# A nine-stage transformer program on one core: retention heads moved into the gate slots, and the first weights and x taken in quarters

## The chip, the core and the metric

The program runs on one core of one Trainium2 chip. The time is the device time of one execution in microseconds (us). The kernel before takes 1748.47 us, the median of three runs (1748.13 to 1749.23). The engines are named as the profile names them: PE is TensorE, DVE is VectorE, ACT is ScalarE, POOL is GpSimd, SP is SyncE, which only starts transfers here.

## The reference

Two models run one after the other on 256 tokens of 1024 features, in float32: two layers (stages F0, A, F1 and F2, B, F3), a final norm (N), and then one layer of a second model with 16 extra tokens in front (R and F4). The stage that changes is the mixer R of the second model:

```python
def _mixer(u, w_in, decay_f, decay_b, gn_w, w_ret_out, q_norm_w, w_uq, kv_norm_w, w_uk, w_uv, w_mla_out, w_o, ...):
    proj = u @ w_in
    rq, rk, rv, rg, a_cq, a_ckv, a_kr, a_gret, a_gmla = jnp.split(proj, SPLIT_IDX, axis=-1)
    rq = _apply_rope(rq...); rk = _apply_rope(rk...) * (RET_DK ** -0.5)
    y_ret = _head_group_norm(_bidir_retention(rq, rk, rv, decay_f, decay_b), gn_w)   # 8 heads of 128 values
    y_ret = (jax.nn.silu(rg) * y_ret) @ w_ret_out
    c_q = _rmsnorm(a_cq, q_norm_w);   q = c_q @ w_uq         # 8 heads: 64 plain and 32 turned features
    c_kv = _rmsnorm(a_ckv, kv_norm_w); k_nope = c_kv @ w_uk; v = c_kv @ w_uv
    y_mla = _mla_attention(q_nope, q_rope, k_nope, k_rope, v) @ w_mla_out
    merged = jax.nn.sigmoid(a_gret) * y_ret + jax.nn.sigmoid(a_gmla) * y_mla
    return merged @ w_o

def _head_group_norm(y, w):   # per token and head
    mu = mean(y); var = mean((y - mu) ** 2)
    return (y - mu) * lax.rsqrt(var + 1e-5) * w
```

The two-sided retention is one product here: scores of all keys against all queries, times a decay that is exp(-a * distance) on one side and exp(b * distance) on the other.

## The kernel before, in words

**Weights.** All weights pass through four slots of SBUF in one fixed order. Slot `g` takes one DMA of up to 1 MB (`load_slot`, L263), then ACT rounds it to a high part (`round_slot`, `whi`, L275) and DVE forms what is left (`rest_slot`, `wlo`, L284). Products are made of three terms, high by high, high by low and low by high (`slot_blocks`, L304), so a slot of 8 row blocks by 256 columns is 48 matmuls of 256 columns. The semaphores `w_landed`, `w_hi`, `w_lo` and `w_used` count slots. `ahead.to(g)` on ACT and DVE says up to which slot they have prepared at that point of their program.

**Order.** Every engine runs a list written out by hand, stage by stage. There is no scheduler; an engine that waits holds all behind it.

**Start.** ACT issues the vectors and x in four DMAs, which count on one semaphore, `l_x`. DVE waits for all four and then lets the scaled x (`u`, high part on ACT L357, low part on DVE L369) be made. SP loads slot 0 whole, then waits for x before slot 1.

**Stage R.** It has 24 input slots: 0 to 7 give q, k and v of the retention, 8 to 11 the latent q and kv and the shared rotary key, 12 to 15 the gate `r_srg` (Silu), 16 to 19 `r_gr` and 20 to 23 `r_gm` (Sigmoid). In each of the last eight slots one retention head runs after the projections of the slot: three products for the scores (L1665), a decay of the scores on DVE (L1913, L1914), three products for the output (L1599, `head_output`), feature by token. The decay `r_W` is made by POOL (L1582), DVE (L1905) and an Exp on ACT (L1812). After the last slot come the statistics of all heads: features lie on partitions, so the mean and the variance are products with a matrix of 1/128 (`meanw`, L1679 and L1690), with a subtraction, a square, a root, a reciprocal of 128 by 256 (L1976), two scalings and a split per head between them. Then two slots of `w_uq` (L322 to L324), the rotation of the queries (L1703), the slots of `w_uk` and `w_uv`, and a loop over the 8 attention heads. In turn h of this loop PE makes scores (L1746), one block of `w_ret_out` (24 matmuls, L1735 to L1737) into the one PSUM bank 7, transposes the softmax (L1754) and multiplies by the values (L1764). DVE does the row maximum (L2026), the reciprocal and scaling (L2037, L2040) and the copy of the transposed softmax (L2045); ACT does Exp (L1859). Then come four slots of `w_mla_out`, the merging of the two branches and four slots of `w_o`.

## Time and profile before

| | us |
|---|---|
| median of three runs | 1748.47 |
| the profiled execution, its own time | 1743.97 |
| span of that execution | 1742.2 |
| PE busy | 1590.9 (91%) |
| DVE busy | 1140.4 (65%) |
| ACT busy | 776.1 (45%) |
| POOL busy | 98.1 (6%) |

Busy time is the union of an engine's instructions, so overlapping matmuls count once. The profiled execution is 4.5 us below the median of the runs. The granted clock of PE, averaged over the span, is 0.953 of full speed. In the rows, x6 counts instructions; one product of float32 data is two matmul instructions, one of rounded data a single one.

### The profile page before, as it was taken

Reading aid. Unit: us, or ns where it says so; the run is one execution under the profiler, and the core shown is the slowest. Engines: PE = TensorE matmul, PEld = TensorE weight load, DVE = VectorE, ACT = ScalarE, POOL = GpSimd, SP = SyncE. Lnnn points to the kernel's source line nnn. Section 1 sums busy time; section 2 is a strip of 40 time slices with the busy share of each in tenths; the row PEclk is TensorE's granted clock in tenths of the full one; section 3 lists DMA queues with packets and bytes.
Section 4 is the critical chain, followed back from the end, with each engine's and each line's share of the span. In section 5 each row is a group of like instructions: output and inputs, shape, how many; then the busy total and the mean of one; then the engine's idle time right before and its main releaser. Section 6 shows DMA issues by size and latency. Waiting matters only on the chain.

```text
span 1742.2 us, 24928 instructions
## 1 busy us (share of the span) xinstructions
PE 1590.9 (91%) x9892; PEld 1399.0 (80%) x9892; DVE 1140.4 (65%) x1324; ACT 776.1 (45%) x910; POOL 98.1 (6%) x92
## 2 busy tenths in 40 slices
PE   5999998889899999999977999998999578799997
PEld 5888898669788888888865888878988367688886
DVE  6876588465367766777567577757565664568764
ACT  5444475312254445444445444434367332354442
POOL 1000200120000000000100000012012000000001
PEclk9999998899899999999989999999999688899999
DMA  7555665200055556554731365474542021355552
GB/s 251 181 171 179 192 187 164 85 1 1 1 169 193 163 169 223 190 182 135 245 122 63 108 193 181 146 227 127 180 132 89 11 73 49 118 174 180 172 182 68
DMA packets 243832, 247.24 MB, mean 142 GB/s; under 512 B 4928, under 2 KB 242256, under 8 KB 243760
## 3 DMA queue, kind: packets, MB, share of 16 engines
q1 hardware_dynamic: 242064, 242.89, 43.8%
q0 software_dynamic: 976, 2.16, 0.4%
q10 hardware_dynamic: 720, 1.17, 0.2%
q8 instruction: 51, 0.84, 0.2%
q14 instruction: 21, 0.17, 0.0%
HBM read 245.16 MB, written 1.05 MB: 141 GB/s over the span
## 4 chain that ended last, share of the span: by engine, by line
PE 77%; DVE 11%; ACT 7%; issue 3%; DMA 1%; POOL 1%; ACTq 0%; DVEq 0%; POOLq 0%
PE ps L318 35%; PE ps L319 18%; PE ps L322 4%; PE ps L323 3%; ACT whi L282 3%; PE ps L324 3%; DVE wlo L288 3%; PE ps L918 1%; PE ps L931 1%; PE ps L884 1%; PE ps L1764 1%; PE ps L958 1%; PE ps L1599 1%; ACT u L357 1%; PE ps L1665 1%
## 5 line engine op out<-in xcount | busy, mean ns | idle before, releaser
L318 PE MATMUL ps<-u,whi 128*128 128x512 f32 x1760 | 625.9, 399 | 29.5 <-DVE u L369 29.5
L288 DVE TENSOR_TENSOR wlo<-raw,whi 128x2048 fp32r<-128x2048 f32 (+3 forms) x261 | 535.2, 2082 | 159.7 <-ACT whi L282 159.7
L319 PE MATMUL ps<-u,wlo 128*128 128x256 f32 x1760 | 499.3, 284 | 0.0
L282 ACT ACTIVATE whi<-raw 128x2048 fp32r<-128x2048 f32 (+3 forms) x261 | 439.5, 1721 | 61.6 <-PE ps L319 49.7
L318 PEld LDWEIGHTS ps<-u,whi 128*128 128x128 f32 x1760 | 334.5, 190 | 108.3 <-issue 16.5
L319 PEld LDWEIGHTS ps<-u,wlo 128*128 128x128 f32 x1760 | 336.3, 191 | 0.1
L318 PE MATMUL ps<-h,whi 128*128 128x512 f32 x880 | 308.1, 394 | 0.0
L319 PE MATMUL ps<-h,wlo 128*128 128x256 f32 x880 | 247.5, 281 | 0.0
L322 PE MATMUL ps<-u,whi 128*128 128x256 f32 (+1 forms) x680 | 198.0, 291 | 9.7 <-DVE u L369 9.7
L318 PEld LDWEIGHTS ps<-h,whi 128*128 128x128 f32 x880 | 165.4, 188 | 38.0
L323 PE MATMUL ps<-u,whi 128*128 128x256 f32 (+1 forms) x680 | 195.6, 288 | 0.0
L324 PE MATMUL ps<-u,wlo 128*128 128x256 f32 (+1 forms) x680 | 195.1, 287 | 0.0
L319 PEld LDWEIGHTS ps<-h,wlo 128*128 128x128 f32 x880 | 166.1, 189 | 0.0
L322 PEld LDWEIGHTS ps<-u,whi 128*128 128x128 f32 x680 | 131.6, 194 | 14.2 <-issue 9.9
L324 PEld LDWEIGHTS ps<-u,wlo 128*128 128x128 f32 x680 | 131.3, 193 | 0.0
L323 PEld LDWEIGHTS ps<-u,whi 128*128 128x128 f32 x680 | 131.1, 193 | 0.3
L464 ACT ACTIVATE gate_a<-gate_s 128x512 f32<-128x512 f32 x55 | 34.7, 632 | 196.3 <-DVE gate_s L477 196.3
L479 DVE TENSOR_TENSOR up_s<-ps,up_s 128x512 f32<-128x512 f32 x55 | 38.0, 692 | 105.0 <-ACT up_s L466 105.0
L380 POOL TENSOR_TENSOR sq<-sq 128x512 f32<-128x512 f32 (+1 forms) x20 | 30.1, 1503 | 1225.4 <-ACT sq L361 1225.1
L357 ACT ACTIVATE u<-x,vec 128x256 fp32r<-128x256 f32 (+1 forms) x64 | 29.1, 502 | 130.9 <-DVE x L517 81.4
L460 ACT ACTIVATE gate_s<-ps 128x512 f32<-128x512 f32 x55 | 32.9, 598 | 71.8 <-PE ps L319 71.8
L515 DVE SCALAR_TENSOR_TENSOR x<-ps,x 128x512 f32<-128x512 f32 x20 | 13.8, 692 | 74.2 <-PE ps L319 74.2
(336 smaller groups left out, 1953.0 us busy)
## 6 DMA issues: line engine op xcount, KB each, us to landing
raw<-in_ffn_w_gu SPq DMA_DIRECT2D x88, 1024.0 KB, 5.7
raw<-in_ffn_w_down SPq DMA_DIRECT2D x32, 768.0 KB, 5.2
raw<-in_w_in SPq DMA_DIRECT2D x22, 1024.0 KB, 5.3
raw<-in_ffn_w_down SPq DMA_DIRECT2D x32, 640.0 KB, 4.4
raw<-in_a_w_in SPq DMA_DIRECT2D x16, 1024.0 KB, 6.2
raw<-in_w_ffn_gate SPq DMA_DIRECT2D x11, 1024.0 KB, 5.4
raw<-in_w_ffn_up SPq DMA_DIRECT2D x11, 1024.0 KB, 6.4
raw<-in_b_w_in SPq DMA_DIRECT2D x6, 1024.0 KB, 7.2
```

The source lines that it names most:

```text
L282: nc.scalar.activation(whi[:, s, 0:n], raw[:, s, 0:n], ACT.Copy).then_inc(w_hi, 1)
L288: nc.vector.tensor_tensor(wlo[:, s, 0:n], raw[:, s, 0:n], whi[:, s, 0:n].bitcast(F32), ALU.subtract).then_inc(w_lo, 1)
L318: nc.tensor.matmul(o, whi[:, s, w], both, start=(first and k == 0), stop=False)
L319: ins = nc.tensor.matmul(o[:, 0], wlo[:, s, w], both[:, 0], start=False, stop=(last and k == nk - 1))
L322: nc.tensor.matmul(o, whi[:, s, w], hi, start=(first and k == 0), stop=False)
L323: nc.tensor.matmul(o, whi[:, s, w], lo, start=False, stop=False)
L324: ins = nc.tensor.matmul(o, wlo[:, s, w], hi, start=False, stop=(last and k == nk - 1))
L357: ins = nc.scalar.activation(uhi[:, k, tok], x[:, k, tok], ACT.Copy, scale=vec[:, w0 + k:w0 + k + 1])
L380: nc.gpsimd.tensor_tensor(sq[:, 0:2, tok], sq[:, 0:2, tok], sq[:, 2 * c:2 * c + 2, tok], ALU.add).then_inc(s_fold, 1)
L460: nc.scalar.activation(gate_s[:, :, tok], ps[:, b0:b0 + 2, SEQ:], ACT.Copy).then_inc(s_low, 1)
L464: nc.scalar.activation(gate_a[:, :, tok], gate_s[:, :, tok], ACT.Silu).then_inc(s_act, 1)
L479: nc.vector.tensor_tensor(up_s[:, :, tok], ps[:, b0 + 2:b0 + 4, 0:SEQ], up_s[:, :, tok], ALU.add).then_inc(s_up, 1)
```

## The change

**Slots of stage R.** The two `w_uq` slots stand among the last input slots. There are still 24 projections; `IN_R` counts these.

```diff
-def mixer_r_in_slots():
-    s = slots_of_in("w_in_2", list(range(C_RQ, C_RQ + 8 * WIDE, WIDE)))
-    s += [("w_in_2", 0, KB, C_CQ, WIDE), ("w_in_2", 0, KB, C_CQ + WIDE, Q_RANK - WIDE), ("w_in_2", 0, KB, C_CKV, WIDE),
...
-def mla_slots():
...
+def mixer_r_slots():
+    row = lambda c, wide=WIDE: ("w_in_2", 0, KB, c, wide)
+    gm, uq = [row(C_GMLA + WIDE * i) for i in range(4)], [("w_uq_2", 0, 3, 384 * i, 384) for i in range(2)]
+    s = [row(C_RQ + WIDE * i) for i in range(8)]
+    s += [row(C_CQ), row(C_CQ + WIDE, Q_RANK - WIDE), row(C_CKV), row(C_KR, P)]
+    s += [row(C_RG + WIDE * i) for i in range(4)] + [row(C_GRET + WIDE * i) for i in range(4)]
+    s += [gm[0], gm[1], uq[0], gm[2], uq[1], gm[3]]
+    return s + [("w_uk_2", 0, 2, 0, 512), ("w_uv_2", 0, 2, 0, 512)]
```

**Start.** Slot 0 comes in four DMAs, each with its own semaphore; each quarter of x has its own too. ACT and DVE take weights and x quarter by quarter, PE goes through the rows in the order in which they land (`first_blocks`: two row blocks, both column blocks, then the next two). ACT's first instruction is a copy of one element. Slots 1 to 3 are loaded once the quarter of the same number is there, no longer after all of x. POOL waits for the quarters of x and raises `s_x`.

```diff
+            if g == 0 and not per:
+                src = dram[name].rearrange("(k p) n -> p k n", p=P)
+                for j in range(PARTS):
+                    dst = raw[:, 0, part(j)].rearrange("p (k n) -> p k n", k=2)
+                    sp.dma_start(dst, src[:, 2 * j:2 * j + 2, bass.ds(c0, wide)]).then_inc(w_landed[j], 16)
+                return
+            if g < SLOTS and not per:
+                sp.wait_ge(w_landed[s], 16)
...
             for name in KEPT:
                 pool.dma_start(kept[name][:, :], dram[name]).then_inc(l_ones, 16)
             pool.dma_start(conv[:, :], dram["vectors"][:, VEC_N:]).then_inc(la_tab, 16)
+            for c in range(4):
+                pool.wait_ge(l_x[c], 16)
+                nc.gpsimd.memset(eps_t[:, 4 + c:5 + c], 0.0).then_inc(s_x, 1)
 
...
+            for c in range(PARTS):
+                dve.wait_ge(w_hi, c + 1)
+                nc.vector.tensor_tensor(wlo[:, 0, part(c)], raw[:, 0, part(c)], whi[:, 0, part(c)].bitcast(F32),
+                                        ALU.subtract).then_inc(w_lo, 1)
+                low_part(dve, stages[0], c)
...
+            nc.scalar.activation(eps_t[:, 8:9], eps_t[:, 3:4], ACT.Copy)
+            act.wait_ge(l_vec, 16)
+            for c in range(PARTS):
+                act.wait_ge(w_landed[c], 16)
+                nc.scalar.activation(whi[:, 0, part(c)], raw[:, 0, part(c)], ACT.Copy).then_inc(w_hi, 1)
+                scaled_high(act, stages[0], c)
```

**Decay and tables.** The tables are loaded before POOL folds the squares of stage R, and the distance table is split into its positive and its negative part. Both factors of the decay are now Exp on ACT; POOL multiplies them. POOL also multiplies the queries by the cosine.

```diff
+        def r_tables(pool):
...
+            for n in r_tab:
+                pool.dma_start(r_tab[n][:, :], dram[n]).then_inc(sr["tab"], 16)
+            pool.dma_start(r_past[:, :, :].rearrange("p a b -> p (a b)"), dram["r_past"]).then_inc(sr["tab"], 16)
+            pool.wait_ge(s_x, 4 * norm_no["N" if "N" in stages else "R"] + 4)
+            pool.dma_start(r_next[:, :, :].rearrange("p a b -> p (a b)"), dram["r_next"]).then_inc(sr["tab"], 16)
...
+        def r_pool(pool):
...
+            def head_decay(h):
+                pool.wait_ge(sr["wx"], h + 2)
+                nc.gpsimd.tensor_tensor(r_W[:, h % 2, :, QT], r_W[:, h % 2, :, QT], r_e[:, :, QT], ALU.mult).then_inc(sr["w"], 1)
...
+            for c in range(2):
+                pool.wait_ge(sr["kr"], c + 1)
+                pool.wait_ge(sr["qrot"], c + 1)
+                q4 = r_qc[rr, 4 * c:4 * c + 4, QT]
+                nc.gpsimd.tensor_tensor(q4, q4, cos, ALU.mult).then_inc(sr["kr"], 1)
```

**Heads in the gate slots.** Head h runs in slot 12 + h, with its scores ahead of the first column block, its output between the two. The output is token by feature now: six products of 128 columns, and the statistics run along the free axis on DVE (`bn_stats`, `bn_aggr`), with one root and one reciprocal for all heads. The normed heads are turned back by transposes.

```diff
+            def heads_turn(i):
+                pe.wait_ge(sr["yn"], i + 1)
+                if i >= 1:
+                    pe.wait_ge(sr["y"], 2 * i)
+                for e in range(2):
+                    for u in range(2):
+                        c = e * SEQ + u * P
+                        ins = nc.tensor.transpose(ps[:, 3, c:c + P], r_o[:, y_of(2 * i + e), u * P:u * P + P], ident[:, :])
+                ins.then_inc(sr["yt"], 1)
...
+            for m in range(HEAD0, IN_R):
+                h, g = m - HEAD0, in_slot(m)
...
+                if h < RH:
+                    scores(h)
+                block_part(g, 0, projected(m)[:, 0], uhi, ulo)
...
+                if m == 21 or m == 22:
+                    heads_turn(2 * m - 41)
+                if h < RH:
+                    head_output(h)
+                block_part(g, 1, projected(m)[:, 1], uhi, ulo).then_inc(w_used, 1)
+                if m == 20:
+                    heads_turn(0)
+                if m == 21 or m == 22:
+                    c = m - 21
+                    if c == 0:
+                        pe.wait_ge(sr["cl"], 3)
+                        pe.wait_ge(sr["sd"], RH)
                     else:
-                        pe.wait_ge(sr["sd"], h)
...
-            for h in range(RH + 1):
-                if h == 1:
-                    head_output(RH - 1)
-                if h < RH:
-                    pe.wait_ge(sr["yc"], h + 1)
-                    if h >= 4:
-                        pe.wait_ge(sr["yd"], h - 3)
-                    nc.tensor.matmul(ps[:, 4 + h % 4, QT], meanw[:, :], r_y[:, y_of(h), QT], start=True,
-                                     stop=True).then_inc(sr["mu"], 1)
-                if h >= 1:
...
-                        pe.wait_ge(sr["yc"], RH)
-                    nc.tensor.matmul(ps[:, g % 4, QT], meanw[:, :], r_ysq[:, g % 2, QT], start=True,
-                                     stop=True).then_inc(sr["var"], 1)
...
-            for c in range(2):
-                slot_blocks(pe, gu + c, [ps[0:MQK, 4 * c + b, QT] for b in range(4)], (r_cqh, r_cql), widths=[MQK] * 4, tok=QT)
...
+                        pe.wait_ge(sr["y"], RH)
+                    slot_blocks(pe, g + 1, [ps[0:MQK, 2 * c + b // 2, (b % 2) * SEQ:(b % 2) * SEQ + SEQ] for b in range(4)],
+                                (r_cqh, r_cql), widths=[MQK] * 4, tok=QT)
+                if m == 21:
+                    heads_turn(2)
```

**ACT.** Sigmoid and Silu are written with Tanh of half the argument; the constants 1 and 0.5 are folded into DVE's and ACT's later instructions.

```diff
+            def decay_parts(h):
+                if h >= 1:
+                    act.wait_ge(sr["w"], h)
+                if h >= 2:
+                    act.wait_ge(sr["sd"], h - 1)
+                nc.scalar.activation(r_W[:, h % 2, :, QT], r_past[:, :, :], ACT.Exp, scale=r_lg[:, 0, h:h + 1])
+                nc.scalar.activation(r_e[:, :, QT], r_next[:, :, :], ACT.Exp, scale=r_lg[:, 1, h:h + 1]).then_inc(sr["wx"], 1)
...
+                    act.wait_ge(sr["o"], h)
+                    act.wait_ge(sr["s"], min(h + 1, RH))
+                    nc.scalar.activation(r_o[:, y_of(h - 1), 0:SEQ], ps[:, 2 + (h - 1) % 2, 0:SEQ], ACT.Copy).then_inc(sr["oc"], 1)
+                if h == RH:
+                    act.wait_ge(sr["bn"], 2 * RH)
+                    nc.scalar.activation(r_rs[:, :, :], r_mv[:, :, :, 1], ACT.Sqrt, bias=eps_t[:, 1:2]).then_inc(sr["sdv"], 1)
+                if h >= RH + 1:
+                    high_heads(h - RH - 1)
+                act.wait_ge(sr["in"], m + 1)
+                if m == 20:
+                    act.wait_ge(sr["cn"], 2)
+                n = (m - 12) % 4
+                dst = (r_srg if m < 16 else r_gr if m < 20 else r_gm)[:, 2 * n:2 * n + 2, QT]
+                nc.scalar.activation(dst, r_t[:, m % 2, :, QT], ACT.Tanh, scale=0.5).then_inc(sr["act"], 1)
+                if m == 22 or m == 23:
+                    query_copy(m - 22)
```

**DVE.**

```diff
+            def head_moments(h):
+                dve.wait_ge(sr["o"], h + 1)
+                for u in range(2):
+                    ins = nc.vector.bn_stats(r_bn[:, h, u, :], ps[:, 2 + h % 2, u * P:u * P + P])
+                ins.then_inc(sr["bn"], 1)
+                dve.wait_ge(sr["bn"], 2 * h + 1)
+                for u in range(2):
+                    ins = nc.vector.bn_aggr(r_mv[:, h, u, :], r_bn[:, h, u, :])
+                ins.then_inc(sr["bn"], 1)
+
+            def normed_heads(i):
+                dve.wait_ge(sr["rs"], 1)
+                dve.wait_ge(sr["oc"], RH)
+                for h in (2 * i, 2 * i + 1):
+                    for u in range(2):
+                        o = r_o[:, y_of(h), u * P:u * P + P]
+                        ins = nc.vector.tensor_scalar(o, o, r_mv[:, h, u, 0:1], r_rs[:, h, u:u + 1], ALU.subtract, ALU.mult)
+                ins.then_inc(sr["yn"], 1)
+
+            def gated_heads(i):
+                dve.wait_ge(sr["yt"], i + 1)
+                dve.wait_ge(sr["sg"], i + 1)
+                for e in range(2):
+                    h = 2 * i + e
+                    nc.vector.scalar_tensor_tensor(r_srg[:, h, QT], ps[:, 3, e * SEQ:e * SEQ + SEQ], r_hw[:, h:h + 1], r_srg[:, h, QT],
+                                                   ALU.mult, ALU.mult).then_inc(sr["y"], 1)
...
+            def gate_of(m):
+                n = m - HEAD0
+                dve.wait_ge(sr["act"], n + 1)
+                s2 = r_srg[:, 2 * n:2 * n + 2, QT]
+                nc.vector.scalar_tensor_tensor(s2, s2, 1.0, r_t[:, m % 2, :, QT], ALU.add, ALU.mult).then_inc(sr["sg"], 1)
...
+            for m in range(HEAD0, IN_R):
+                h = m - HEAD0
+                if h < RH:
+                    decayed_scores(h)
+                if 13 <= m <= 16:
+                    gate_of(m - 1)
+                if m == 20:
+                    dve.wait_ge(sr["sdv"], 1)
+                    nc.vector.reciprocal(r_rs[:, :, :], r_rs[:, :, :]).then_inc(sr["rs"], 1)
+                    normed_heads(0)
+                if m == 21:
+                    normed_heads(1)
+                    gated_heads(0)
+                if m == 22:
+                    normed_heads(3)
+                    gated_heads(2)
+                if m == HEAD0:
...
+                ahead.to(in_slot(m) + 3)
+                if h < RH:
+                    head_moments(h)
+                if m == 21:
+                    gated_heads(1)
+                    heads_rest(0)
+                    normed_heads(2)
+                if m == 22:
+                    heads_rest(1)
+                    gated_heads(3)
+                if m == 23:
+                    heads_rest(2)
```

**Attention loop.** The block of `w_ret_out` alternates between two PSUM banks and is cut in two, with the values of the head before in the middle; the transposes of a head stand at the end of its own turn.

```diff
-                pe.wait_ge(w_lo, g + 1)
...
-            for h in range(MH + 2):
-                if h < MH:
...
-                    ins.then_inc(sr["sm"], 1)
-                    retention_block(h)
-                if 1 <= h <= MH:
-                    g = h - 1
-                    pe.wait_ge(sr["p"], g + 1)
...
+            for h in range(MH):
...
+                if h >= 1:
+                    pe.wait_ge(sr["p"], h)
...
+                ins.then_inc(sr["sm"], 1)
+                retention_part(h, 0, KB // 2)
+                if h >= 1:
+                    weighted_values(h - 1)
+                ins = retention_part(h, KB // 2, KB)
+                ins.then_inc(w_used if h % 2 else sr["rot"], 1)
+                pe.wait_ge(sr["p"], h + 1)
...
+                for t, (j0, nj) in enumerate(TILES):
+                    for u in range(2):
...
+                ins.then_inc(sr["pt"], 1)
+            weighted_values(MH - 1)
```

**What stands in a row on the engines.** ACT in one of the eight head slots, before (a turn in slots 16 to 23; `whi` is the rounding of a later weight slot, `r_q` the copied head output):

```order
L282 ACTIVATE whi<-raw 128x2048
L1783 ACTIVATE r_q<-ps 128x256
L1812 ACT_TABLE_LOAD
L1812 ACTIVATE r_W<-r_W 128x3x256
L1817 ACT_TABLE_LOAD
L1817 ACTIVATE r_gr<-r_t 128x2x256
```

and now (a turn in slots 12 to 19):

```order
L294 ACTIVATE whi<-raw 128x2048
L1890 ACTIVATE r_W<-r_past,r_lg 128x3x256
L1891 ACTIVATE r_e<-r_next,r_lg 128x3x256
L1937 ACTIVATE r_o<-ps 128x256
L1948 ACTIVATE r_gr<-r_t 128x2x256
```

The two table loads of each head are gone and a second Exp of 128x768 has come in.

DVE in one head slot, before:

```order
L288 TENSOR_TENSOR wlo<-raw,whi 128x2048
L1913 SCALAR_TENSOR_TENSOR r_s<-ps,r_W 128x2x256
L1914 SCALAR_TENSOR_TENSOR r_s<-ps,r_W 16x256
L1905 SCALAR_TENSOR_TENSOR r_W<-rt_r_dist,r_lg,r_e 128x3x256
L1941 TENSOR_TENSOR r_t<-ps,rstd 128x2x256
```

and now, in the slot that has the most of it (slot 15: the gate and one reciprocal are in it too):

```order
L2013 SCALAR_TENSOR_TENSOR r_s<-ps,r_W 128x2x256
L2014 SCALAR_TENSOR_TENSOR r_s<-ps,r_W 16x256
L2076 SCALAR_TENSOR_TENSOR r_srg<-r_srg,r_t 128x2x256
L300 TENSOR_TENSOR wlo<-raw,whi 128x2048
L2020 BN_STATS r_bn<-ps 128x6 x2
L2024 BN_AGGR r_mv<-r_bn 128x2 x2
L2124 RECIPROCAL r_csd<-r_csd 128x256
L2070 TENSOR_TENSOR r_t<-ps,rstd 128x2x256
```

The decay exponents have left DVE; the statistics, the gate and the reciprocal of the latent norms stand between the weights' low part and the eviction `r_t`.

PE behind the last input slot, before (`r_q` holds the heads, `meanw` the matrix of 1/128, `r_cqh` the latent queries):

```order
L1599 MATMUL ps<-r_s,r_v 128x256 x3
L1679 MATMUL ps<-r_q,meanw 128x256
L1690 MATMUL ps<-r_ysq,meanw 128x256
L1679 MATMUL ps<-r_q,meanw 128x256
L1690 MATMUL ps<-r_ysq,meanw 128x256 x2
L322 MATMUL ps<-r_cqh,whi 96x256
```

and now, at the end of slot 20 and the start of slot 21:

```order
L1674 MATMUL ps<-u_53,whi 128x256
L1675 MATMUL ps<-u_53,wlo 128x256
L1708 MATMUL ps<-ident,r_o 128x128 x4
L1673 MATMUL ps<-u_53,whi 128x256
L1674 MATMUL ps<-u_53,whi 128x256
```

The 16 products with `meanw` are gone; 16 transposes of 128x128 in four groups stand between projections.

## Rows read from the trace of the kernel before

**Rows 1.** Page, busy time and share of the span of PE.

```profile
PE 1590.9 (91%) x9892; PEld 1399.0 (80%) x9892; DVE 1140.4 (65%) x1324; ACT 776.1 (45%) x910; POOL 98.1 (6%) x92
```

**Rows 2.** Windows of 10 us: busy us by engine, PEclk, DMA share, GB/s.

```profile
1250.00:1260.00 10.00, 10.00 (x84) 10.00 (x83) 6.38 (x5) 4.78 (x5) 0.00 (x0) 1.00 0.78 254
...
1360.00:1370.00 10.00, 5.06 (x12) 3.09 (x12) 6.36 (x8) 3.67 (x8) 0.00 (x0) 0.57 0.00 1
...
1430.00:1440.00 10.00, 6.26 (x36) 5.45 (x35) 4.87 (x9) 3.62 (x8) 0.00 (x0) 0.83 0.15 52
...
1490.00:1500.00 10.00, 9.07 (x31) 5.95 (x30) 1.65 (x2) 1.33 (x2) 0.00 (x0) 0.50 0.20 59
```

**Rows 3.** Chain that ended last, in stage R: start us, us, what.

```profile
1268.84 2.21 PE ps L1653 x10
...
1306.46 1.59 PE ps L1665 x6
...
1315.63 1.59 PE ps L1665 x6
...
1371.98 1.76 DVE r_sd L1976
...
1390.45 0.53 PE ps L322
...
1401.42 1.85 PE ps L1703 x8
...
1431.20 0.67 PE ps L1754 x6
...
1443.51 1.11 PE ps L1746 x4
...
1448.12 1.59 PE ps L1764 x6
...
1495.37 0.58 PE ps L322
...
1543.83 0.79 PE ps L318
```

**Rows 4.** Groups by line, 1200 to 1600 us: count, busy us, mean ns, idle before.

```profile
L288 DVE TENSOR_TENSOR wlo<-raw,whi 128x2048 fp32r<-128x2048 f32 (+2 forms) x48 | 99.2, 2079 | 60.7 <-ACT whi L282 60.7
...
L1817 ACT ACT_TABLE_LOAD x10 | 12.8, 1283 | 0.2
...
L1812 ACT ACT_TABLE_LOAD x8 | 10.3, 1283 | 0.1
...
L1859 ACT ACTIVATE r_p<-ps,r_st 128x272 f32<-128x272 f32 x16 | 7.7, 483 | 24.2 <-DVE r_st L2028 24.2
...
L1812 ACT ACTIVATE r_W<-r_W 128x768 f32<-128x768 f32 x8 | 6.8, 845 | 17.6 <-DVE r_W L1905 17.6
...
L2026 DVE TENSOR_REDUCE r_st<-ps 128x2 f32<-128x544 f32 x8 | 5.8, 721 | 5.5 <-PE ps L1746 5.5
...
L2045 DVE COPY r_pt<-ps 128x512 f32<-128x512 f32 x8 | 5.5, 692 | 18.8 <-PE ps L1754 18.8
```

**Rows 5.** Groups by line and form, PE, 160 to 700 us (stage A).

```profile
L918 PE MATMUL ps<-a_X,a_LT 128*128 128x128 f32 x192 | 26.2, 282 | 0.2 <-DVE a_X L1183 0.2
```

**Rows 6.** Timeline of POOL, 1140 to 1200: start us, us, what.

```profile
1157.19 1.30 POOL L380 TENSOR_TENSOR sq<-sq 128x512 f32<-128x512 f32 x1 [14.09 <-ACT sq L361]
...
1179.96 4.61 POOL L380 TENSOR_TENSOR sq<-sq 128x544 f32<-128x544 f32 x2 [19.52 <-ACT sq L361]
```

**Rows 7.** Timeline of DVE from 1184 us.

```profile
1184.79 2.85 DVE L288 TENSOR_TENSOR wlo<-raw,whi 128x2048 fp32r<-128x2048 f32 x1
```

**Rows 8.** Timeline of the first 24 us.

```profile
16.49 0.77 PE L318 MATMUL ps<-u,whi 128*128 128x512 f32 x1 [16.49 <-DVE u L369]
```

**Rows 9.** Chain in the first 60 us.

```profile
25.60 1.29 PE ps L393 x6
```

**Rows 10.** The four DMAs of x (L621), from issue to landing.

```profile
DMA to landing us min/median/max: 6.6/7.5/7.6
```

More of the change, by code:

```diff
@@ L257, in build, with part @@
         w_used = sem("w_used")
+        PARTS = 4
+        MORE = PARTS - 1
+        def part(j):
+            return slice(2 * j * WIDE, 2 * (j + 1) * WIDE)
         def elems(g):
@@ L271, in load_slot @@
             sp.dma_start(dst, src).then_inc(w_landed[s], 16)
-            if g == 0 and not per:
-                sp.wait_ge(l_x, 64)
         def round_slot(act, g, i=None, per=0, n=None):
@@ L448, in glu_products @@
             rhs = (u2,)
-            slot_blocks(pe, g, [halves(b0 + b) for b in range(2)], rhs, i=i, per=per, tok=tok, ready=ready)
+            if g == 0 and i is None:
+                first_blocks(pe)
+            else:
+                slot_blocks(pe, g, [halves(b0 + b) for b in range(2)], rhs, i=i, per=per, tok=tok, ready=ready)
             if between:
@@ L1607, in r_pe @@
+            for m in range(HEAD0):
+                if m >= 3:
                     pe.wait_ge(sr["in"], m - 2)
[L1608 to L1611 removed]
                 b0 = in_bank(m)
@@ L1942, in r_dve @@
+            def gate_of(m):
[3 more added lines that the diff above has]
+                nc.vector.scalar_tensor_tensor(s2, s2, 1.0, r_t[:, m % 2, :, QT], ALU.add, ALU.mult).then_inc(sr["sg"], 1)
+            for m in range(HEAD0):
+                ahead.to(g0 + m + 3)
+                evicted(m)
                 if 1 <= m <= 4:
```

646 lines of the change are left out of this document (317 added, 329 removed), and 6 rows, old and new, of the table sr.

## The prediction

> **What bounds the kernel now.** I read the busy shares first: PE works 91% of the span [rows 1], so outside a few places only fewer or faster products would help. The windows show where those places are [rows 2]. At 1250 to 1260 PE is full: 84 matmuls in 10 us, 0.119 each, so an input slot of 48 costs 5.7 us. At 1360 to 1370 PE is busy 5.06 of 10 at a granted clock of 0.57, that is mostly at the 1.2 GHz level. At 1430 to 1440 it is busy 6.26 at 0.83; at 1490 to 1500 it is full again but still at 0.50, after the idle time ahead of it. Then I followed the chain of waits through stage R [rows 3]. Up to the last input slot it runs on PE: one head slot starts at 1306.46, the next at 1315.63, a period of 9.17. Behind them the chain goes over ACT and DVE, head by head, with a reciprocal of 1.76 in each, until 1390.45, when the products of `w_uq` start. These last to 1401.42; the first transposes of the attention loop come at 1431.20, the first product of `w_mla_out` at 1495.37, the next stage at 1543.83. These points are my yardsticks. The start is a second place: PE has nothing before 16.49 [rows 8], and the sums of squares between slot 0 and slot 1 run from 25.60 to 26.9 [rows 9].
>
> **Start.** Slot 1 begins at 26.9 now. Of x, a DMA lands 6.6 to 7.6 us after its issue [rows 10], and the issues begin in the second microsecond, so I put the first quarter at 8. By then its quarter of the weights is there. From 8 on ACT needs about 1.45 for a quarter (a rounding of a quarter of 1.9, two scaled copies), so the last scaled quarter is done at 13.5 to 14 and DVE's low part at 14.5. PE starts at about 10 with two row blocks and is through slot 0 at 17. The sums wait for POOL, which folds pairs at 1.30 each [rows 6] behind the squares, which are now behind all scaled copies: about 18.2, and 1.3 for the sums. Slot 1 is rounded after the squares and has its low part at 19.5 too. So slot 1 starts at 19.5 instead of 26.9: **7.4 gained**. Bounds: 4 if the fourth quarter of x comes 3 later because slot 1 is loaded beside it, 9 if the sums don't wait. Behind it PE has been full, so the shift stays.
>
> Here a rule of the Trainium skill speaks against the change. The four DMAs of x land 6.6, 7.5 and at most 7.6 after their issues, though they are issued one behind the other, so whatever is fixed in one overlaps with the others [rows 10]. "DMA: Bandwidth & Descriptors", section "Anatomy of one DMA", gives about 2.0 us of fixed cost to every DMA, on POOL's path. By it, were the four paid one behind the other, the last quarter would land some 6 us later and the start would gain about 1. The trace doesn't agree with that for x.
>
> **Stage R up to the loop.** In before, L1653 starts at 1268.84 behind slots 12 and 13 [rows 3], so slot 12 starts at 1268.84 - 11.4 = 1257.4. To the first transposes it is 1431.2 - 1257.4 = 173.8. Now:
> - eight slots with a head. The scores are the same products; the output is 12 instructions of 128 columns instead of 6 of 256. A float32 128x128 group takes 26.2/192 = 0.136 an instruction [rows 5], so 1.63, what the six take. Period 9.17, 8 x 9.17 = 73.4. Bound: if an instruction of 128 costs as much as one of 256 now (0.28), +1.7 a head, +13.
> - four slots without: 22.8. The sums of L1653: 2.2. Both `w_uq` slots, 72 matmuls at 0.119: 8.6. Sixteen transposes at 0.67/6 = 0.11: 1.8.
> - what the norm still makes PE wait. Root and reciprocal are one each for all heads, but the root is in ACT's row behind a rounding and 1.28 of table load [rows 4], and the transposes of heads 2 and 3 need the gating of heads 0 and 1, behind 2.1 of low part. I take 3.1; bounds 0 and 8.
> - the stretch from 1401.42 to 1431.20, 29.8. Half of the rotation goes to POOL and the heads' rest is spread, but DVE now has in a row a low part, the sines, a copy of the key, the sum, two copies of the keys, sines, sum and another low part before it can take the first maximum. I leave it at 29.8; bounds 22 (PE's own work and the first softmax) and 34.
> Sum 73.4 + 22.8 + 2.2 + 8.6 + 1.8 + 3.1 + 29.8 = 141.7, so **32.1 gained**. Nothing is left of 16 products with `meanw`, which ran at the low clock.
>
> Cover of the head slots. DVE: low part 2.1, scores 1.0, eviction 0.69 (as L2045, 128x512), gate 0.7 in four, a reciprocal of 1.76 in two, and the statistics, which no row shows: two reads of 128x128, between a quarter of an eviction (0.17) and half a reciprocal (0.88), plus two tiny ones; I take 0.8 in all, at most 2.4. That makes 4.6 to 7.1, at most 8.7, under 9.17. ACT: 1.9 of rounding, two Exp at 0.845, a copy and a Tanh of 0.6: 4.6, and the 18 table loads of 1.283 are down to a handful [rows 4]. POOL: a product of 128x768; by the row of 1.30 for 512 it takes 1.95, by the row under a busy DVE (4.61 for two of 544) 3.3 [rows 6]. It is made a head ahead, so its 3.3 are hidden until ACT and POOL together pass 9.17. That the tables land earlier is worth under one and counted as nothing.
>
> The contention is the second place where a rule matters. DVE's low part takes 2.85 while POOL folds [rows 7] and 2.08 on the mean [rows 4], and POOL takes 2.3 instead of 1.3 [rows 6]: both lose about a microsecond when they overlap. "GPSIMD Engine Reference", section "Specifications", says that the two share SBUF interfaces and contend where DVE reads two inputs from SBUF, as the low part does; the trace agrees. Before, POOL's instruction in the head slots had one such input.
>
> **Loop.** From 1431.20 to 1495.37 it is 64.2. PE's work in a turn is 24 x 0.119 = 2.86, scores 1.11, transposes 0.67, values 1.59 [rows 3]: 6.2, with the gaps 6.35. The ring from one softmax to the next is transposes 0.67, scores 1.11, maximum 0.72, its scaling 0.2, two Exp with their sums 1.36, reciprocal 0.16 and two scalings 0.72, 4.9 and some 0.3 of hand-overs: it fits under PE's work, since the two banks let PE run on and a turn no longer ends with a wait for the copy (0.69). In turns 1 and 3 a rounding and a low part of 2048 stand in the ring: +1 each. So 7 x 6.35 + 2 + 3.9 (last transposes, copy, values, high and low part) = 50.4, **13.8 gained**. Bounds: 8 us less gain, if every turn pays a low part's wait of one, 2 more.
>
> **Tail.** The first slot of `w_mla_out` runs at the 1.2 GHz level now: 24 matmuls take 5.5. At the full clock 2.9: **2.6 gained**, if PE came in busy. The rest (merging, `w_o`, update of x) goes at the pace of rounding, low part and update and stays.
>
> Sum: 7.4 + 32.1 + 13.8 + 2.6 = 55.9. The profiled execution takes 1743.97, 1.8 around its span of 1742.2; 1743.97 - 55.9 = 1688.1. It stands 4.5 under the median of the runs, so the forecast for the median is 1748.5 - 55.9 = 1692.6.
>
> **Rivals.**
> - *DVE and POOL in each other's way.* The overlap costs DVE and POOL a microsecond each in every head slot, the statistics cost 2.4, and slots 15 to 18, with the reciprocals and the latent norms, go over 9.17; PE then pays about 1.4 a head, 11: 1704. For it: rows 6 and 7. Against: 2 us of slack in most slots.
> - *The clock comes back.* The stretch before the loop falls to 22, the norm's waits are covered, the start gains 9: 10 to 13 more, 1681. For it: 0.57 and 0.50 in rows 2 are idle time's doing. Against: the DVE row above.
> - *The start gains nothing*, since x is the last to come anyway: 1700. Against: ACT, DVE and PE work in a row of 17 us behind the last x now.
> - *Slower:* the ring from eviction over Tanh, rounding (1.9), two Exp (1.7), POOL (3.3), the scores on DVE (1.0) and the output on PE is not a head ahead but closed within a slot, with DVE's 8.7 and PE's 3.2 in it. A head slot would be 0.6 + 1.9 + 1.7 + 3.3 + 8.7 + 3.2 = 19.4, 10.2 more, 82 for eight: 1692.6 + 82 = 1774. It decides at 9.17 + 55.9/8 = 16.2 a slot. Against: `r_W` has two buffers, and ACT makes head h + 1 during head h.
>
> **Numbers.** My forecast 0.55 (own range 1684 to 1700), DVE and POOL 0.17, the clock 0.20, the start 0.05, slower 0.03. The range takes in the bounds of the output products (+13) and of the stretch before the loop (-8): 1677 to 1708. A measurement of this kernel tells 0.2% from no change. Faster by more 0.96, within 0.01, slower by more 0.03.
>
> **What would show it.** Right: second slot's first product at 19 to 20; head slots of 9.2 with PE full from slot 12 to the end; no window under 0.9 of PE busy for the norm; 110 to 114 us from slot 12 to the end of slot 23; under ten table loads in stage R; a turn of the loop at 6.3 to 6.5, near 7.3 in two of them; a full clock in the loop. Wrong: head slots over 10 with PE waiting for `r_s`; `r_W` on POOL ending after the scores; PE waiting for `r_o` or `r_srg` in slots 21 and 22 for more than 8 together; turns of 8 or more.

## The result and the profile after

| | before | after |
|---|---|---|
| median of four runs, us | 1748.3 | 1689.7 (1688.8 to 1690.3) |
| profiled execution, its own time | 1743.97 | 1690.05 |
| its span | 1742.2 | 1688.3 |
| granted clock over the span | 0.953 | 0.965 |

The ratio is 0.967, 95% interval 0.965 to 0.968: 58.6 us less, where 55.9 were forecast. Two further kernels, one with the old start and one with the old stage R, split this into 5 for the start (7.4 forecast) and about 55 for stage R (48.5 forecast).

The busy shares of the page after, against [rows 1]: DVE, ACT and PE do nearly as much as before in a shorter span.

```profile
PE 1577.3 (93%) x9924; PEld 1397.9 (83%) x9924; DVE 1123.8 (67%) x1344; ACT 754.4 (45%) x888; POOL 105.4 (6%) x99
```

Windows of 10 us of the kernel after (columns as in [rows 2]): a head slot, the norm, the stretch before the loop (two), the loop, the tail.

```profile
1300.00:1310.00 10.00, 10.00 (x72) 8.57 (x72) 6.90 (x10) 4.78 (x7) 2.28 (x1) 1.00 0.23 61
1340.00:1350.00 10.00, 6.83 (x57) 6.44 (x57) 8.98 (x17) 4.49 (x5) 0.00 (x0) 1.00 0.14 53
1380.00:1390.00 10.00, 7.58 (x20) 5.30 (x21) 8.64 (x8) 2.03 (x4) 1.22 (x1) 0.69 0.12 41
1390.00:1400.00 10.00, 7.00 (x40) 6.06 (x39) 4.68 (x8) 2.73 (x6) 0.00 (x0) 0.83 0.17 52
1400.00:1410.00 10.00, 10.00 (x65) 7.67 (x65) 6.82 (x14) 4.27 (x10) 0.00 (x0) 1.00 0.17 54
1460.00:1470.00 10.00, 7.24 (x46) 7.03 (x47) 7.77 (x7) 4.56 (x5) 0.00 (x0) 0.83 0.43 140
```

In the head slots PE is full and DVE has 3 of 10 to spare. The window that was at 5.06 busy and 0.57 [rows 2] has no counterpart: up to the end of the loop the worst ones in stage R are the norm, where PE stands for 3.2 at the full clock, and 1380 to 1400, where it stands for 5.4 and the clock falls to 0.69. The loop is full at 1.00.

The chain of waits of the kernel after from slot 20 to the first transposes (start, us, what), which answers to [rows 3]:

```profile
1334.67 0.70 DVE r_t L2070
...
1335.94 1.15 ACT whi L294
1337.09 0.73 ACT r_cqh L1932
1337.82 0.55 ACT r_ckh L1933
...
1338.65 1.28 ACT L1940
1339.95 0.32 ACT r_rs L1940
...
1341.69 1.26 DVE wlo L300
...
1347.02 0.63 PE ps L1708 x4
...
1380.17 2.20 issue
1382.38 1.22 DVE r_qc L2161
...
1389.51 1.81 ACT whi L294
1391.34 2.29 DVE wlo L300
1393.67 0.74 DVE r_st L2186
...
1396.60 1.54 PE ps L1864 x6
```

The eight reciprocals of 1.76 are gone from the chain. In the norm PE stands twice, 1.4 for the normed heads (up to 1341.75) and 1.8 for their gating (up to 1347.02). The chain ahead of both comes from the root (L1940), with its table load of 1.28, behind a rounding and the copies on ACT; between root and gating lies a row of DVE with a low part of 1.26 in it. Behind 1380 the chain is DVE's row: "issue" of 2.20 is its copy of the shared key, and a low part of 2.29 stands ahead of the first maximum.

Where the 53.9 between the two profiled executions lie:

| piece | before | after | gained | forecast |
|---|---|---|---|---|
| span up to R's sums | 1188.58 | 1187.92 | 0.7 | 7.4 |
| R's sums to slot 12 | 68.8 | 67.1 | 1.7 | 0 |
| slot 12 to first transposes | 173.8 | 141.6 | 32.2 | 32.1 |
| to first product of `w_mla_out` | 64.2 | 48.2 | 16.0 | 13.8 |
| to F4's first product | 48.5 | 46.0 | 2.5 | 2.6 |
| to F4's sums | 6.0 | 5.2 | 0.9 | 0 |

From F4's sums to the end it is 192.4 in both. Of the signs named ahead of the result these came: PE full in the head slots, six table loads behind R's start (under ten), a loop at the full clock. Its turns of 6.2 are a little under the 6.3 to 6.5 named, and no two of them are at 7.3. These didn't: slot 1 at 19 to 20 (21.2), head slots of 9.2 (9.6), slot 12 to the end of slot 23 in 110 to 114 (116.2), no norm window under 0.9 (0.68).

### The profile page after: what moved, and what is told of

It reads as the page before. It is cut to its first block, busy times and chain, and to the rows that moved or that the text cites. A ratio compares the mean times of both kernels' runs of the same rounds, so it can differ in the third digit from the quotient of the medians.

```text
span 1688.3 us, 25007 instructions
## 1 busy us (share of the span) xinstructions
PE 1577.3 (93%) x9924; PEld 1397.9 (83%) x9924; DVE 1123.8 (67%) x1344; ACT 754.4 (45%) x888; POOL 105.4 (6%) x99
## 4 chain that ended last, share of the span: by engine, by line
PE 80%; DVE 10%; ACT 6%; issue 3%; DMA 1%; POOL 0%; SPq 0%; ACTq 0%; DVEq 0%; POOLq 0%
PE ps L330 36%; PE ps L331 18%; DVE wlo L300 3%; ACT whi L294 3%; PE ps L334 3%; PE ps L335 3%; PE ps L336 3%; PE ps L1673 2%; PE ps L1674 2%; PE ps L1675 2%; PE ps L966 1%; PE ps L979 1%; PE ps L932 1%; PE ps L1697 1%; PE ps L1006 1%
## 5 line engine op out<-in xcount | busy, mean ns | idle before, releaser
L330 PE MATMUL ps<-u,whi 128*128 128x512 f32 x1744 | 616.9, 398 | 9.9 <-DVE u L390 9.9
L331 PE MATMUL ps<-u,wlo 128*128 128x256 f32 x1744 | 494.0, 283 | 0.0
L330 PEld LDWEIGHTS ps<-u,whi 128*128 128x128 f32 x1744 | 330.1, 189 | 86.3 <-DVE u L390 11.2
L331 PEld LDWEIGHTS ps<-u,wlo 128*128 128x128 f32 x1744 | 332.7, 191 | 0.2
L334 PE MATMUL ps<-u,whi 128*128 128x256 f32 (+1 forms) x488 | 143.6, 294 | 9.5 <-DVE u L390 9.5
L335 PE MATMUL ps<-u,whi 128*128 128x256 f32 (+1 forms) x488 | 141.7, 290 | 0.0
L336 PE MATMUL ps<-u,wlo 128*128 128x256 f32 (+1 forms) x488 | 141.4, 290 | 0.0
L334 PEld LDWEIGHTS ps<-u,whi 128*128 128x128 f32 x488 | 95.7, 196 | 11.2 <-issue 7.0
L335 PEld LDWEIGHTS ps<-u,whi 128*128 128x128 f32 x488 | 95.3, 195 | 0.2
L336 PEld LDWEIGHTS ps<-u,wlo 128*128 128x128 f32 x488 | 95.4, 196 | 0.0
L553 DVE SCALAR_TENSOR_TENSOR x<-ps,x 128x512 f32<-128x512 f32 x20 | 13.8, 692 | 74.2 <-PE ps L331 74.2
```

What stands on the lines that cost most here:

```text
L330: nc.tensor.matmul(o, whi[:, s, w], both, start=(first and k == 0), stop=False)
L331: ins = nc.tensor.matmul(o[:, 0], wlo[:, s, w], both[:, 0], start=False, stop=(last and k == nk - 1))
L334: nc.tensor.matmul(o, whi[:, s, w], hi, start=(first and k == 0), stop=False)
L335: nc.tensor.matmul(o, whi[:, s, w], lo, start=False, stop=False)
L336: ins = nc.tensor.matmul(o, wlo[:, s, w], hi, start=False, stop=(last and k == nk - 1))
```

## Experiments

Each was timed in five rounds (twelve for the two kernels near the kernel before: old R with the new start, and Tanh) beside the kernel before; ratios are to that kernel. Its median was 1746.3, 1744.4 and 1746.0 in the three sets, with single runs from 1741 to 1754. The third set (the heads' output, Tanh, the entry to the loop, all three edits) ran on another chip. Differences of 2 or 3 us between two versions can't be told from the times; there I go by the length from R's sums to F4's in the profiles, which is 308.0 in the changed kernel and 309.1 in its rerun.

**The changed kernel again.**

> The changed kernel once more, as the yardstick of this chip. All theories: 1690 (1688 to 1691), ratio 0.966 to 0.968.

1686.6, ratio 0.965 (0.963 to 0.968), runs from 1682.6 at a clock of 0.969 to 1690.6 at 0.962. The median is under the 1688 to 1691 that I expected, and the time of one kernel moves over 8 us, roughly with its clock.

**Start and stage R apart.** The first kernel has R changed and the old start, the second the old R and the new start.

```diff
-        MORE = PARTS - 1
+        MORE = 0
...
+            if g == 0 and not per:
+                sp.wait_ge(l_x, 64)
...
-            if g == 0 and i is None:
-                first_blocks(pe)
-            else:
-                slot_blocks(pe, g, [halves(b0 + b) for b in range(2)], rhs, i=i, per=per, tok=tok, ready=ready)
+            slot_blocks(pe, g, [halves(b0 + b) for b in range(2)], rhs, i=i, per=per, tok=tok, ready=ready)
```

> Stage R as changed, the start as before. Theory 'given back': the 7.1 us that the first sums come earlier are lost again in stages F0 and A (0.7 are left at R's sums), so this is the changed kernel plus 0 to 1.5: 1690 to 1692. Rival (the prediction's term): the shift stays and the start is worth 7.4, so this takes 1697, and stage R is worth 48.5. Slot 1's first product is back at 26.9 in both, R's sums at 1188 (given back) or 1195 (rival).

> Stage R as before, the start as changed. Theory 'given back': the kernel before less 0 to 1.5: 1747 to 1748, that is under what a measurement can tell. Rival: 7.4 less, 1741. The first sums come at 18.3 in both; the theories part at stage A's sums (206 against 203) and at R's.

With the old start: 1691.8, ratio 0.969 (0.966 to 0.971). With the old R: 1741.6, ratio 0.997 (0.996 to 0.999), that is 4.7 less than before, 1.7 to 7.7. So stage R is worth 54.5 (old start) or 55.0 (new start), and the start 5.3 or 4.7: they add. "Given back" (0 to 1.5) falls, narrowly, by the second kernel; that the first lies in its 1690 to 1692 says nothing, since the changed kernel took 1686.6 beside it and not 1690. The rival's 7.4 is still inside the interval, and only the profiles below speak against it. "Given back to 0.7" came from one pair of profiles, and the profiled executions of the changed kernel are the second longest of four and the longest of five. Over all profiled executions, three with the old start and eight with the new one as it is, the means of the points at which the sums of squares start are:

| | first sums | stage A's | F1's | R's |
|---|---|---|---|---|
| old start | 26.1 | 210.9 | 499.3 | 1189.8 |
| new start | 18.5 | 205.6 | 495.3 | 1186.8 |
| gained | 7.6 | 5.3 | 4.0 | 3.1 |

The 7.6 are there at the first sums. 2 go before stage A. Chain of the kernel after, first 24 us, and windows of 5 us:

```profile
9.97 0.63 ACT whi L692
10.60 0.80 ACT u L374 x2
11.40 1.05 ACT sq L382 x2
12.53 1.30 POOL sq L401
13.97 1.29 POOL sq L401
15.33 2.88 POOL sq L404
18.34 2.90 PE ps L414 x6
```

```profile
15.00:20.00 5.00, 1.66 (x4) 1.42 (x5) 4.40 (x2) 3.23 (x3) 3.12 (x2) 0.75 1.10 348
20.00:25.00 5.00, 5.00 (x18) 4.16 (x18) 4.41 (x4) 4.40 (x5) 0.00 (x0) 0.57 1.10 348
25.00:30.00 5.00, 5.00 (x31) 4.40 (x30) 2.28 (x4) 2.30 (x3) 0.00 (x0) 1.00 1.11 351
```

PE stands for 3.8 ahead of the sums, which then run near the 1.2 GHz level, 2.90 where six such instructions took 1.46 in the kernel before (its chain in [rows 9] shows 1.29 of that), and the products of slot 1 up to 25 with them (0.57). Of the other 2.3, 1.3 go in stage A, where the eight profiles with the new start need 288.8 to 290.8 from its sums to F1's and the three with the old one 288.1 to 289.0. The clock falls at other places there: from 290 to 300 it is 0.70 after and 0.99 before. The eight fall into two groups. In four (the changed kernel, its rerun, the old R, the cosine on DVE) the clock from 15 to 35 is 0.83, stage A takes 290.3 to 290.8, and R's sums start at 1187.3 to 1188.2. In the other four it is 0.91 there, stage A takes 288.8 to 289.2, and R's sums start at 1185.1 to 1186.3. So at R's sums the start is worth 2 in one group and 4 in the other. What puts an execution into one of them stays open; the 5 of the medians, with 1.7 to 7.7 around it, agrees with either.

**The loop with one bank's wait.**

```diff
-                if f >= 2:
-                    pe.wait_ge(sr["gr"], f - 1)
+                if f >= 1:
+                    pe.wait_ge(sr["gr"], f)
```

> The changed kernel, but in the attention loop the block of w_ret_out of turn f waits for the copy of block f-1 instead of f-2, as with one PSUM bank. Theory (the loop gained because a turn no longer ends with that wait and the ring): DVE makes the copy behind the copy of the softmax, so seven turns wait 0.7 to 1.4 each, plus 5 to 10: 1695 to 1700, turns of 7 to 7.6. Rival (the new order of the transposes and values gave the 16 us alone, the second bank nothing): 1690, turns of 6.2.

1700.0, ratio 0.973 (0.971 to 0.976), the upper end of the forecast times, but 13.5 more than the changed kernel beside it, where I had 5 to 10. The chain of one turn of this kernel:

```profile
1414.77 0.66 PE ps L1864 x6
1415.43 0.93 PE ps L1851 x4
1416.38 0.74 DVE r_st L2186
1417.31 0.33 DVE r_gr L2196
1417.69 0.39 PE ps L1673
...
1422.57 0.66 PE ps L1864 x6
```

A turn is 7.8 instead of 6.2, since PE waits for the maximum and then for DVE to read the block (L2196). Six turns cost 1.6 each, 9.7, and the first takes 11.8 instead of 7.8 (9.3 in the rerun). R's sums to F4's are 321.7 against 308.0 and 309.1. In this version the loop takes 61.8, 2.4 less than before the change. So the new order alone gives little, and without the second bank the greater part of the loop's 16.0 is gone.

In the kernel before PE's wait was another one, though. There the clean turns took 6.2 already: the first transposes of the turns start at 1431.0, 1441.1, 1447.3, 1459.9, 1466.3, 1474.7, 1480.9 and 1487.4, that is 10.1, 6.2, 12.6, 6.4, 8.4, 6.2 and 6.5 apart. In the long ones a low part stands in DVE's row ahead of the reading of the block, for which PE waits (8.7 in three waits), and the products behind it start at the low clock. Chain of the kernel before:

```profile
1450.02 1.91 ACT whi L282
1451.95 2.29 DVE wlo L288
1454.25 0.34 DVE r_gr L2022
1454.63 0.58 PE ps L1735
```

With the new order on one bank no turn shows a low part any more (the maximum stands ahead of the reading instead, and all turns are 7.8). So the order takes away the wait for the low part, the second bank the wait that the order brings, and only both give 6.2 in every turn. The old order with two banks was not run.

**Heads' output feature by token**, as before the change; the statistics then run over the wrong axis.

```diff
-                for u in range(2):
-                    i0, c = META + u * P, u * P
-                    for t, (j0, n) in enumerate(TILES):
-                        ins = nc.tensor.matmul(ps[:, 2 + h % 2, c:c + P], r_s[0:n, t, i0:i0 + P],
+                for t, (j0, n) in enumerate(TILES):
+                    ins = nc.tensor.matmul(ps[:, 2 + h % 2, 0:SEQ], r_v[0:n, t, h * RDV:h * RDV + RDV], r_s[0:n, t, QT],
```

> The changed kernel with the heads' output feature by token as before, three products of 256 columns in the place of six of 128 (the statistics then run over the wrong axis). Theory, from the 1.91 of its 12 instructions after and the 1.68 of 6 before: each head slot 0.23 shorter, 9.37 for 9.60, 1.8 over eight and under what the time can tell; if the slots fall by more than 0.3, something else of the new form costs (the copies, the statistics). Rival (a slot is bound by another engine): 9.60 still.

1685.4, ratio 0.965 (0.964 to 0.967): in time not to be told from the changed kernel. In the trace it is plain. Timeline of PE, heads 4 and 5, after and here:

```profile
1305.82 1.66 PE L1685 MATMUL ps<-r_q 64*128 64x256 f32 x6
1310.35 2.07 PE L1697 MATMUL ps<-r_v,r_s 128*128 128x128 f32 x12
1315.39 1.66 PE L1685 MATMUL ps<-r_q 64*128 64x256 f32 x6
```

```profile
1301.58 1.66 PE L1685 MATMUL ps<-r_q 64*128 64x256 f32 x6
1306.12 1.65 PE L1695 MATMUL ps<-r_s,r_v 128*128 128x256 f32 x6
1310.74 1.66 PE L1685 MATMUL ps<-r_q 64*128 64x256 f32 x6
```

The period is 9.16 instead of 9.57: twelve instructions of 128 columns take 0.42 more than six of 256, twice what I expected and a quarter of the bound. Eight heads pay 3.4 for having their statistics on the free axis; R's sums to F4's are 304.6 here, 3.4 less than in the changed kernel.

**Tanh in the kernel before.**

```diff
-                    nc.scalar.activation(dst, r_t[:, m % 2, :, QT], ACT.Silu if m < 16 else ACT.Sigmoid).then_inc(sr["act"], 1)
+                    nc.scalar.activation(dst, r_t[:, m % 2, :, QT], ACT.Tanh).then_inc(sr["act"], 1)
```

> The kernel before, with Tanh in the place of Silu and Sigmoid in stage R's gates (the function alone is changed, so the gates have other values). ACT has no table loads between its Exp and its gates any more: 18 of 1.283, 23 us of ACT's row. Theory (ACT is idle for over half of the head slots, so its tables cost nothing): less by 0 to 2, within what a measurement tells. Rival (the loads stand in the ring of the heads): 5 to 23 less, 1722 to 1741.

1742.6, ratio 0.998 (0.997 to 0.999): 3.5 less, 1.4 to 5.8. That is over my 0 to 2; the rival's 5 is just inside, its 23 far out. The head slots keep their period (1306.37 to 1315.54, 9.17); only the first head's wait of 1.60 for the scores on DVE is down to 0.18. From R's sums to the scores at 1306.37 it is 115.6, against 117.9 in the kernel before: 1.4 of that is this wait, and 0.8 is a wait of the first rotation, which this profile doesn't have. In the kernel with the old R and the new start the same wait of 1.60 is followed by a fall of the clock (0.78 from 1300 to 1310), and it is 120.5. So what that one wait costs depends on the clock behind it, 1.4 in one profile and about 3 more in the other. Behind the first transposes this profile is 3.5 shorter than that of before (0.93 against 0.50 from 1490 to 1500 [rows 2]), but the kernel with the old R and the new start is as short there without Tanh (115.0 against 115.3). Nearly all of ACT's 23 us of table loads lay in time in which nobody waited for ACT.

**Cosine on DVE.**

```diff
-                nc.gpsimd.tensor_tensor(q4, q4, cos, ALU.mult).then_inc(sr["kr"], 1)
+                nc.vector.tensor_tensor(q4, q4, cos, ALU.mult).then_inc(sr["kq"], 1)
```

> The changed kernel with the product of queries and cosine on DVE instead of POOL. Theory 'POOL is the slow member there' (2.2 us of DVE waiting at 1378 to 1381, the same again in the trace of the rerun): DVE has 2 x 0.7 more in its row but no longer waits for POOL's 2.0 each: 1 to 3 us less. Rival (POOL's part lies beside work of DVE, and the wait is for something else): 1 to 2 us more.

1689.3, ratio 0.966 (0.964 to 0.968). Neither theory: R's sums to F4's take 309.1 as in the rerun. I had read the 2.2 of "issue" as a wait for POOL. It is an instruction of DVE, the key's copy. DVE's rows of the kernel after (start, us, line, what), and of a kernel below in which that copy stands elsewhere:

```profile
1378.82 1.29 DVE L2153 TENSOR_TENSOR r_rt<-ps,rt_m_sin 32x512 f32<-32x512 f32 x2
1380.15 2.22 DVE L2166 COPY r_kc<-r_kr 32x2176 f32<-32x2176 f32 x1
1382.38 1.22 DVE L2161 TENSOR_TENSOR r_qc<-r_qc,r_rt 32x1024 f32<-32x1024 f32 x1
```

```profile
1369.07 1.28 DVE L2144 COPY r_kc<-r_kr 32x2176 f32<-32x2176 f32 x1
...
1375.96 1.29 DVE L2154 TENSOR_TENSOR r_rt<-ps,rt_m_sin 32x512 f32<-32x512 f32 x2
1377.35 2.08 DVE L2162 TENSOR_TENSOR r_qc<-r_qc,r_rt 32x1024 f32<-32x1024 f32 x1
```

The copy takes 2.22 beside POOL's product (1378.87 to 1381.22) and 1.28 without it; the sum behind it takes 1.22 without and 2.08 with it. POOL's product costs DVE 0.9, whichever instruction of the two lies beside it (the sine product, with one input in PSUM, takes 1.29 either way). With the product on DVE the copy takes 1.28 in its old place, 0.9 less, and the product itself 1.21 there, so DVE's row is as long as before and so is the whole.

**First sums behind slot 1, root early, and both.**

```diff
-            glu_products(pe, st, 0, between=lambda: sums(pe, st), ready=x_split(st))
+            if g0 == 0:
+                glu_products(pe, st, 0, ready=x_split(st))
+                sums(pe, st)
```

```diff
                 h = m - HEAD0
+                if h == RH:
+                    act.wait_ge(sr["o"], h)
+                    act.wait_ge(sr["s"], RH)
+                    nc.scalar.activation(r_o[:, y_of(h - 1), 0:SEQ], ps[:, 2 + (h - 1) % 2, 0:SEQ], ACT.Copy).then_inc(sr["oc"], 1)
+                    act.wait_ge(sr["bn"], 2 * RH)
+                    nc.scalar.activation(r_rs[:, :, :], r_mv[:, :, :, 1], ACT.Sqrt, bias=eps_t[:, 1:2]).then_inc(sr["sdv"], 1)
                 ahead.to(in_slot(m) + 3)
```

> The changed kernel with the first sums of squares behind slot 1 instead of between the slots 0 and 1. Theory: PE's wait of 3.8 for POOL's last fold goes, slot 1 starts at 17.6 with its low part instead of 21, and the clock isn't lost in between: the first 60 us are 3 to 4.5 shorter, the whole 2 to 4. Rival 'given back' (stage A's waits and clock fall where the lead of the weights decides, not the start): A's sums come 3 earlier, but the whole changes by less than 1.

> The changed kernel with ACT's copy of the last head and the root of the variances ahead of the rounding and the latent high parts in slot 20. Theory: the root is what PE waits for at slot 21 (idle 3.2 at 1340 to 1350), behind a rounding of 1.2 and two copies of 1.3: that idle time falls to 0 to 1, the whole by 2 to 3. Rival (DVE's row of reciprocal, normed heads and low part is what is late, since the rounding comes later now and so its low part): no change, or up to 1 more.

> Both of the edits before this one. Theory: they lie 1300 us apart and add: 4 to 7 less than the changed kernel, 1680 to 1686. Rival: each is given back, 1687 to 1690.

Sums late: 1685.8, ratio 0.9655 (0.964 to 0.967), no difference. Slot 1 starts at 17.8 instead of 21.2, but PE still stands, for 2.5, now for the low part of slot 1, and the clock falls behind that instead (0.74 from 20 to 25). Stage A's sums come at 205.4, 0.5 earlier than in the changed kernel and no earlier than in the second group above, where I had expected 3. Root early: 1684.4, ratio 0.9649 (0.962 to 0.967). In the norm PE's idle time falls from 3.2 to 1.1:

```profile
1340.00:1350.00 10.00, 8.94 (x77) 8.76 (x76) 8.37 (x20) 4.88 (x6) 0.00 (x0) 1.00 0.27 92
```

and R's sums to F4's take 304.9 against 308.0 and 309.1, that is 3.1 to 4.2 less, where I had 2 to 3. 2.1 of it is the norm; the rest lies behind it, where the first turn of the loop takes 6.2 and not 7.8. Both: 1682.2, ratio 0.9634 (0.9615 to 0.9653), in the forecast 1680 to 1686, but by the profile with the root's gain alone, 304.9 again.

**Entry to the loop.**

```diff
             gu = g0 + 26
             gr = gu + 2
+            kr = r_kr[0:ROPE, :].unsqueeze(1).broadcast_to([ROPE, MH, TOK])
+            nc.vector.tensor_copy(r_kc[NOPE:MQK, :, :], kr)
             ahead.to(gu + 3)
...
             gm = gr + 4
-            ahead.to(gr + 2)
```

The second part is done on ACT and on DVE.

> The changed kernel with two things taken out of DVE's row between slot 23 and the first softmax: the copy of the shared key (2.2) stands behind the last eviction, where DVE is idle for 4, and the rounding and low part of the second block slot come behind the first softmax, not ahead of it. Theory (that stretch is bound by DVE's row, and PE waits 3.0 for the first softmax behind that low part): 2.2 and 2 to 3 less, and a loop that comes in at the full clock: 4 to 6 less, 1681 to 1683. Rival (the low part then stands in turns 0 and 1, where it delays the copy of the transposed softmax; the first turns grow by as much): 2 less.

> All three edits at once: the first sums behind slot 1, the root early, the entry to the loop. Theory: they add, 1676 to 1679, ratio 0.959 to 0.962. Rival: what one gives the other had already (a clock that stays up once): 1681 or more.

Entry: 1684.0, ratio 0.9642 (0.962 to 0.966), just over the 1681 to 1683 of the theory; R's sums to F4's 304.9. The first transposes come 205.2 behind R's sums instead of 208.7, the third 218.8 instead of 222.7. The first two turns take 6.96 and 6.65 where later ones take 6.19, which is the rival's growth; but in the changed kernel the first took 7.84, since it came in at the low clock (9.27 in its rerun, 6.25 with the root early). All three: 1680.7 (1678.2 to 1681.5), ratio 0.9623 (0.9604 to 0.9642), R's sums to F4's 301.2. The theory had 1676 to 1679 and the rival 1681 or more: it is between them, with nothing from the first sums and with the root and the entry adding. It is the fastest version, by the ratios 5 to 8 less than the changed kernel, for which the two sets gave 0.9668 (0.9651 to 0.9684) and 0.9653 (0.9627 to 0.9678). Its interval lies below the first of these and overlaps the second; the length of R, 301.2 against 308.0 and 309.1, is the firmer sign.

## Why the prediction held, and where it didn't

*The sum* was right within 3, in part by luck, since two errors cancel in part: the start is worth 5, not 7.4, and stage R about 55, not 48.5. The start's interval (1.7 to 7.7) still holds 7.4; that of R (50.5 to 58.9, from the ratio 0.9687) doesn't hold 48.5.

*Start.* Slot 1's first product came at 21.2, not 19.5. x landed earlier than I put it: POOL sees the last quarter at 10.2, and PE was through slot 0 at 14.5, not 17. But the last fold on POOL took 2.88 beside DVE's low part, where I had 1.30 from [rows 6]. These two balance by chance, the sums start at 18.3 where I had 18.2, and nearly all of the 1.7 is the sums at the low clock, 2.90 for 1.3. The step that failed is "behind it PE has been full, so the shift stays": behind a wait of 3.8 PE ran at the low level, and stage A, which isn't full, took some more in half of the profiles.

*Head slots.* The term was 73.4 at 9.17; the period is 9.57: an instruction of 128 columns took 0.159 (1.91 for twelve) and not the 0.136 of [rows 5], and the six of 256 take 1.49 in the chain of the version above, not 1.63. That is 0.4 a head, 3.2 in all. PE was full and DVE, with bn_stats at 0.49 a pair and bn_aggr at 0.25, had room; so DVE and POOL in each other's way did not decide, though POOL's product took 2.2, between my 1.95 and 3.3.

*Norm.* 3.1 forecast, 3.2 measured, and for the reasons given, root and table load behind a rounding (a wait of 1.4) and the gating behind a low part (1.8): moving the root took 2.1 of the two away.

*Stretch before the loop.* "I leave it at 29.8" was 4.4 too much (25.4), which by luck paid for the head slots and 1.1 more up to the end of slot 23; hence 141.6 against 141.7. It is DVE's row as listed, and moving two of its members took 3.5 more.

*Loop.* The turn of 6.2 is PE's work, as worked out. "In turns 1 and 3 +1 each" was wrong: low parts fall into DVE's idle time there and no turn shows them. The gaps of 0.15 that I had added aren't there either. It is one turn of 7.8, while the clock comes up, six of 6.19 and 3.2 behind: 48.2 for 50.4. The first turn alone moves this by 1.5 either way between executions and versions (9.27, 6.25). And "a turn no longer ends with a wait for the copy (0.69)" names too small a wait: before, it was the reading of the block behind a low part, 8.7 in three turns.

*Tail.* 2.6 forecast, 2.5 measured, and for the reason given: the first 24 matmuls of `w_mla_out` take 3.0 at the full clock (1444.80 to 1447.83).

*What I had at nothing:* 1.7 between R's sums and slot 12, of which 0.8 is a wait of the first rotation for DVE. DVE stood for 3.2 there for an Exp of ACT on the decay's parameters (L1786), and ACT from 1191.9 to 1195.3 for their DMA, the last of nine tables that POOL issues from 1185.4 to 1190.2. After the change they are there in time and ACT goes on at 1191.3. This is "that the tables land earlier is worth under one", and the rest of the 1.7 stays open. And 0.9 at F4's start, where the clock is up.

*From profile to runs.* Stage R gains 53.3 in this pair of profiles and 54.5 to 55.0 by the medians. Single profiled executions of one R differ by 1 to 2 in its length (before 361.3, with the new start 359.0; changed 308.0 and 309.1), so the last one or two are not settled. Against the forecast of 48.5, the 53.3 are 2.2 more in the loop and 2.6 in the two terms at nothing.

## What to carry to other kernels

Look for what stands *ahead* of an instruction in its engine's row, not only for what it waits for: the root, the key's copy and a low part that was needed two turns later each held up PE, and moving them took 7 off stage R without any less work. A second bank is worth as much as the wait that it breaks, and that depends on the row: the maximum and the reading cost 1.6 in a turn of the new order, a low part ahead of the reading 2 to 6 in every second turn of the old one. A gain of a few us at the start is known only from the medians of many runs, since clock and waits behind it move by as much.
